# Spreading the expert gates in two fp16 parts of the gate times 2^15 instead of three bf16 parts

## What is computed

```
q = xt @ w_q; s = q . sub_keys                       # 8 heads, two halves, 128 keys each
s1, i1 = top_k(s[:, :, 0], 16); s2, i2 = top_k(s[:, :, 1], 16)
top_s, pos = top_k(s1 + s2, 16)                      # 16 experts of 128*128, per token and head
gate = softmax(top_s)
act = gelu(u[idx] . xt)
out = sum over (head, k) of gate * act * v[idx]
```

## Time and profile before

| | us |
|---|---|
| median of 3 runs | 4196.76 (4195.95 to 4196.98) |
| profiled execution | 4202.15 |
| span of its trace | 4200.4 |
| PE busy / PEld busy | 3752.2 / 3136.2 |
| DVE busy / ACT busy / POOL busy | 2165.0 / 1513.3 / 1956.9 |
| spread_gates, first panel's products to last gate store issued | 720.17 to 961.14 |

### The profile page before, as it was taken

How to read it: one execution, slowest core, us unless ns; L and a number is a source line. 1 busy time by engine, 2 the same in 40 slices (tenths; PEclk the granted TensorE clock), 3 DMA queues, 4 the chain that set the end, 5 groups by cost and what they waited for, 6 DMA issues and landing times. The chain is left out here.

```text
span 4200.4 us, 51711 instructions
## 1 busy us (share of the span) xinstructions
PE 3752.2 (89%) x17668; PEld 3136.2 (75%) x17668; DVE 2165.0 (52%) x3388; ACT 1513.3 (36%) x2617; POOL 1956.9 (47%) x1517
## 2 busy tenths in 40 slices
PE   6948998998899999999979875999979997569999
PEld 5526998998899999988868523788768885247887
DVE  4663598884899867643225235433333321644330
ACT  3322455663333333544223313333233421333332
POOL 3724576334688777555415101454435543004544
PEclk9979999998999999999989866999989998679999
DMA  3002354457999989433323100223223336003332
GB/s 115 20 17 84 113 172 143 151 193 269 363 406 405 373 328 352 168 100 95 93 88 98 45 0 25 86 94 95 89 62 99 94 93 132 0 1 95 91 94 91
DMA packets 172780, 570.20 MB, mean 136 GB/s; under 512 B 15457, under 2 KB 58593, under 8 KB 155140
## 3 DMA queue, kind: packets, MB, share of 16 engines
q1 hardware_dynamic: 152244, 427.68, 31.0%
q0 software_dynamic: 20432, 141.31, 9.0%
HBM read 518.85 MB, written 50.07 MB: 135 GB/s over the span
## 5 line engine op out<-in xcount | busy, mean ns | idle before, releaser
L267 POOL TENSOR_TENSOR weight_low<-weight_ring,weight_high 128x512 fp32r<-128x512 f32 x1264 | 1714.2, 1378 | 1855.0 <-ACT weight_high L239 1358.6
L281 PE MATMUL banks<-normed_high,weight_high 128*128 128x512 f32 (+1 forms) x2592 | 976.7, 377 | 84.5 <-PEq L390 43.9
L282 PE MATMUL banks<-normed_low,weight_high 128*128 128x512 f32 (+1 forms) x2592 | 968.8, 374 | 0.0
L239 ACT ACTIVATE weight_high<-weight_ring 128x512 fp32r<-128x512 f32 x632 | 399.0, 631 | 1325.9 <-PE banks L288 1224.5
L281 PEld LDWEIGHTS banks<-normed_high,weight_high 128*128 128x128 f32 x2592 | 499.1, 193 | 159.2 <-issue 73.5
L288 PE MATMUL banks<-normed_high,weight_low 128*128 128x512 f32 (+1 forms) x2592 | 589.3, 368 | 6.8 <-POOL weight_low L267 6.6
L282 PEld LDWEIGHTS banks<-normed_low,weight_high 128*128 128x128 f32 x2592 | 498.0, 192 | 64.6 <-issue 1.5
L288 PEld LDWEIGHTS banks<-normed_high,weight_low 128*128 128x128 f32 x2592 | 474.0, 188 | 71.8 <-POOL weight_low L267 10.5
L241 ACT ACTIVATE weight_high<-weight_ring 128x512 fp32r<-128x512 f32 (+1 forms) x632 | 389.4, 616 | 78.3 <-PE banks L288 77.6
L281 PE MATMUL banks<-parked_high,weight_high 128*128 128x384 f32 x768 | 261.9, 341 | 16.0 <-ACT weight_high L239 10.4
L1742 DVE TENSOR_TENSOR square<-square,banks 128x512 f32<-128x512 f32 x88 | 60.5, 687 | 416.5 <-PE banks L288 414.9
(11 more groups left out here) (364 smaller groups left out, 5801.8 us busy)
## 6 DMA issues: line engine op xcount, KB each, us to landing
weight_ring<-in_experts SPq DMA_DIRECT2D x256, 512.0 KB
weight_ring<-in_ffn_gate SPq DMA_DIRECT2D x88, 512.0 KB
weight_ring<-in_ffn_up SPq DMA_DIRECT2D x88, 512.0 KB
weight_ring<-in_ffn_down SPq DMA_DIRECT2D x64, 512.0 KB
expert_gates<-spread_space SPq DMA_DIRECT2D x6, 4096.0 KB, 12.2
parked_space<-expert_gates SPq DMA_DIRECT2D x24, 768.0 KB
parked_space<-parked_activations SPq DMA_DIRECT2D x24, 768.0 KB
weight_ring<-in_a_w_in SPq DMA_DIRECT2D x28, 512.0 KB
```

The costliest lines, as they stand in the source:

```text
L239: m.nc.scalar.activation(m.w_hi[:, s % PARTS, 0:HALF], m.ring[:, s, 0:HALF], ACT.Copy).then_inc(m.half_high, 1)
L267: m.nc.gpsimd.tensor_tensor(m.w_lo[:, s % PARTS, at], m.ring[:, s, at], m.w_hi[:, s % PARTS, at].bitcast(FP), ALU.subtract).then_inc(done, 1)
L281: m.nc.tensor.matmul(out, w_hi, hi(c), start=(first and c == 0), stop=False)
L282: m.nc.tensor.matmul(out, w_hi, lo(c), start=False, stop=False)
```

## The change

Gates are multiplied by 2^15 and written as two fp16 parts: the rounding, and what it leaves. Every two-byte tile of the stage becomes fp16 instead of bf16. The PE then sums two products per token instead of three, DVE multiplies `hot1` twice instead of three times, and ACT's eviction takes a scale of 2^-15. The scratch `rest` goes.

```diff
-BF = mybir.dt.bfloat16
+HF = mybir.dt.float16
...
-GATE_PARTS = 3
+GATE_PARTS = 2
+GATE_UP = 2.0 ** 15
...
-        rest = space.take(2, DENSE)
...
-        keys16 = m.tensor("spread_keys", BATCH, P, dt=BF, ctx=ctx)
+        keys16 = m.tensor("spread_keys", BATCH, P, dt=HF, ctx=ctx)
...
-                for k in range(GATE_PARTS):
-                    m.vector_order.step(dve, nc.vector.tensor_copy(gate16[:, k, :], value))
-                    if k < GATE_PARTS - 1:
-                        m.vector_order.step(dve, nc.vector.tensor_tensor(rest[:, k, :], value, gate16[:, k, :],
-                                                                         ALU.subtract))
-                        value = rest[:, k, :]
+                m.vector_order.step(dve, nc.vector.tensor_scalar(gate16[:, 0, :], value, GATE_UP, None, ALU.mult))
+                m.vector_order.step(dve, nc.vector.scalar_tensor_tensor(
+                    out=gate16[:, 1, :], in0=value, scalar=GATE_UP, in1=gate16[:, 0, :], op0=ALU.mult, op1=ALU.subtract))
...
                             nc.scalar.activation(out.rearrange("p a t -> p t a"),
                                                  m.bank[4 + b][:, :].rearrange("p (t a) -> p t a", t=BATCH),
-                                                 ACT.Copy).then_inc(evac, 1)
+                                                 ACT.Copy, scale=1.0 / GATE_UP).then_inc(evac, 1)
```

More of the change, by code:

```diff
@@ L1014, in spread_gates @@
     with ExitStack() as ctx:
-        space = Space(m, ctx, "spread", 2 * KEYS * SPREAD_T + 2 * DENSE + SLOTS * DENSE + TT * HEADS + KEYS)
+        space = Space(m, ctx, "spread", 2 * KEYS * SPREAD_T + SLOTS * DENSE + TT * HEADS + KEYS)
         stage = [space.take(KEYS, SPREAD_T) for h in range(2)]
-        rest = space.take(2, DENSE)
         buffers = space.take(SLOTS, DENSE)
@@ L1020, in spread_gates @@
         number = space.take(KEYS)
-        keys16 = m.tensor("spread_keys", BATCH, P, dt=BF, ctx=ctx)
[L1023 to L1027, removed]
+        keys16 = m.tensor("spread_keys", BATCH, P, dt=HF, ctx=ctx)
+        index16 = m.tensor("spread_indices", 2, DENSE, dt=HF, ctx=ctx)
+        gate16 = m.tensor("spread_gate_parts", GATE_PARTS, DENSE, dt=HF, ctx=ctx)
+        hot2 = m.tensor("spread_hot2", 2, PAIR * BATCH * P, dt=HF, ctx=ctx)
+        hot1 = m.tensor("spread_hot1", 2, PAIR * BATCH * P, dt=HF, ctx=ctx)
+        rows1 = m.tensor("spread_rows1", 2, GATE_PARTS, PAIR * BATCH * P, dt=HF, ctx=ctx)
         keys_by_token = keys16.rearrange("p t a -> p (t a)").rearrange("p (a t) -> p a t", t=BATCH)
```

## The result

The changed kernel takes 4154.91 us in the median of 4 runs (4150.26 to 4163.36); the kernel before, measured beside it, 4196.87 (4195.95 to 4201.9). The ratio is 0.9895, with a 95% interval of 0.9883 to 0.9907. The gain is 42 and 44 us. The forecast was 4152.3, with a range of 4148 to 4166.

What follows compares the result with a forecast made beforehand. The prediction took PE (TensorE) to bound the spreading stage: 16 matmuls fewer at 0.1158 us in each of 24 panels make 44.5 us, other terms nothing, so 4196.8 - 44.5 = 4152.3 us, with a range of 4148 to 4166.

Steps and rivals of the forecast that it cites:

- TensorE sets the pace: In the spreading stage PE is busy 20.00 of 20.00 us and the other engines wait for it.
- 16 x 0.1158 = 1.853 us a panel, 44.5 in all: PE's spreading: 16 of 48 matmuls go per panel, each giving back its whole distance, over 24 panels.
- Types and scale cost nothing: ACT's evictions with a scale and copies to two-byte tiles: no added time, 592 ns scaled against 597 plain.
- D: Rival: fp16 loses DVE its fast form (4236 us), or PE loads it as slowly as float32 (4209); chance 0.05.
- DVE's loop, 7.62 against 8.03: Two-buffer loop per panel: DVE's way 7.62 us, PE's 8.03, leaving 0.4, so POOL's slip of 1.97 costs nothing.
- B: Rival: POOL blocks DVE longer, PE waits for rows 3 to 15 us in all, 4156 to 4167; chance 0.12.
- ACT's evictions don't pile up: PE's batch shrinks to 0.93 us, still over the 0.90 between ACT's evictions.
- The start is hidden, nothing won: Stage start: DVE is done some 1.3 us sooner, but PE's first load waits for ACT's split, so no gain.
- C: Rival: in PE's spreading a removed matmul is worth only 0.060 us, 23 us in all, 4174; chance 0.02.
- The median: Whole kernel: forecast median of 4152.3 us, from 4196.8 less 44.5.

Runs made afterwards that it cites:

- e4: Kernel before to changed for DVE alone: two sets of rows, TensorE still doing 12 matmuls a batch; 4200.29 us, ratio to before 0.9992.
- e2: The changed kernel with three fp16 parts instead of two, types and scale kept; 4200.53 us, ratio to the kernel before 0.9993.
- e3: The changed kernel with 8 matmuls a batch, but DVE still making a third set of rows that nobody reads; 4171.19 us.
- e5: The changed kernel with DVE's second operation on the gate done three times, so DVE is ready 1.2 us later; 4158.77 us.
- e9: The changed kernel with only the moving operand of the spreading matmuls read as neighbouring columns, mixing up tokens; 4139.89 us.
- e7: The changed kernel with only the stationary operand of the spreading matmuls read as neighbouring columns, mixing up tokens; 4153.61 us.
- e8: The changed kernel with both operands of the spreading matmuls read as neighbouring columns, mixing up tokens; 4142.85 us.
- e10: The changed kernel with two tokens innermost instead of four, same computation; 4140.94 us, ratio to the kernel before 0.9860.
- e12: The kernel before, three bf16 parts, with two tokens innermost instead of four and nothing else; 4167.01 us, ratio 0.9917.

## Why the prediction was right, point by point

- *TensorE sets the pace* was right, and it was so for the reason given: e4 takes DVE's share alone and gains nothing. The rows that told it were the windows and the waits together; a PE at 89% of the span would not have been enough.
- *16 x 0.1158 = 1.853 us a panel, 44.5 in all.* Measured 9.88 - 7.99 = 1.89, and 43.6 + 1.9 = 45.5 in all, 1.0 more than the term; the panel was predicted at 8.03. Dividing the row's 5.56 by its 48 was a little low: PE's row of 48 takes 5.84 and that of 32 takes 3.94, so a removed matmul is worth 1.90/16 = 0.119.
- *Types and scale cost nothing.* Right; e2 shows it for DVE, PE and ACT at once. With that, D is excluded in both of its forms.
- *DVE's loop, 7.62 against 8.03, so the slip is costed at nothing.* Right, and as close as computed: 0.3 us of time in hand where 0.4 were expected, the slip 1.98 where 1.97 was expected. It didn't grow (at most 2.0 in any of the 24 panels), so B didn't come about. e3 shows that the loop is real: with DVE's pair back at 3.23 us the panels are 8.48 apart in the median, 8.68 in the mean. B's price in the prediction left out the falls of the clock that came with TensorE's waits in e3, where the mean panel is 0.2 us over the median.
- *ACT's evictions don't pile up.* Right: four in 3.94 us, and ACT still waits for PE 10.0 us at them.
- *The start is hidden, nothing won.* Wrong, by 1.4 us. The row at 720.17 named ACT's split as the releaser. It was the last event before the load, not the one waited for: the changed kernel's first load starts at 718.17, ahead of that split. The wait was `gt_ready`, which DVE raised behind its fifth operation, and e5 shows it.
- *C, the removed matmuls were cheap* was rightly given little, since the whole distance came back. But the argument against it, that the loads fill the row and so set the price, was not the reason: in e9 they are nearly as long and the price is half. The price was the moving operand's 8-byte distance (e7, e9). The count came out right because every matmul in the row paid it; in that the forecast was lucky. C's own 0.060 a matmul is what one costs with the moving columns 4 bytes apart. The Trainium skill, TensorE: Matmul & The Clock Gate, on the back-to-back issue gap, has 81 ns for 128 columns in a stream of loads and matmuls, and 56 ns for the matmul alone. Neither is this kernel's price. With neighbouring columns e8 comes to 56 (0.90/16), though each of its matmuls has a new load, so here the 81 is too high and the lower figure fits.
- *The median.* 4154.91 for 4152.3; the traces say 46.9 us for the stage, the medians 42 and 44. With runs 10 us apart the difference is not resolved, and a median within 3 us of the forecast is partly luck.

## What to carry to other kernels

Before counting what an engine's removed work is worth, read one period of the loop in the timeline and write down each engine's way round it, buffers included; here 1.89 us from PE counted in full only because DVE also lost 1.2. TensorE's half alone brings 31 of the 44 us (e3), DVE's half alone nothing that the runs could tell (e4). Where an engine that never waited begins to wait, look at its granted clock as well. When a trace names a releaser, look whether the code has that wait there: the last event before a start is not always the one that was waited for. And when a distance between matmuls is longer than elsewhere, ask for its cause before cutting their number: with two tokens innermost instead of four the same computation wins another 14 to 18 us, and half of what the third part cost TensorE in the kernel before was its layout.

## What the runs showed of the hardware

- A matmul of 128 two-byte columns, in a row of such with a new stationary operand each, takes 114 to 116 ns, a row's length by its count, when the moving columns lie 8 bytes apart (3.66 us for 32, 5.57 for 48), 58 ns at 4 bytes (e10, and e12 in bf16), and 56 to 58 at 2 bytes (e8, e9). The stationary operand's distance matters little: 112 ns against 114 (e7: 3.58 us for 32, against 3.66).
- The Trainium skill, SBUF — State Buffer, under Door 1 (the DMA port swizzle), says that accesses stay at full bandwidth while at least two fall into a line of 16 bytes, and gives eight bf16 elements as how far one can stride for free. TensorE's moving operand doesn't agree: two to a line, at 8 bytes, cost double, four to a line nothing. A step of 8 elements wasn't tried.
- DVE's two-byte operations of 128x1024 take the same time with four dimensions and two elements innermost as with four innermost (0.69 us, 0.605 apart), so a layout of pairs costs the writer nothing here.
- In most panels DVE lost 1.98 us to POOL's pair of operations, and POOL took up to 3.4 for what takes 2.53 alone. That slip is a quarter of DVE's time in e10 and the largest thing left there; moving POOL's work off DVE's way was not tried.
- TensorE's granted clock, at the 2.4 GHz level from 723 us to the end of the stage in the changed kernel, falls to the 1.2 GHz level for a few us in kernels where TensorE has to wait: behind a wait of 2.41 us in e10 (its products then start 0.31 us apart instead of 0.17), and three times in e3, behind 0.8 to 1.1. It doesn't follow every wait: 2.28 us at 801.35 in e10 had no fall, nor had the 1.2 to 1.5 in each panel of e12 from 736 on. What decides was not tried.
